# First mixer of a two-layer encoder: query and key blocks by seven half-size products, and GpSimd copies of x by halves

## The chip, the cores and the metric

One NeuronCore of a Trainium2 chip runs the whole kernel. The metric is the device time of one execution, in microseconds (us); less is better.

## The reference

The input x is 256 tokens of 1024 values, float32. Two layers follow, each a mixer with a residual add and then a mixture of experts with a residual add. The change lies in the first mixer, and there in its input projection:

```python
def even_mixer(xn, w_in, q_gain, k_gain, rel_bias, w_out):
    u = xn @ w_in                       # 256 x 1024 times 1024 x 2048
    q, k, v, ub = jnp.split(u, [NA_WIDTH, 2 * NA_WIDTH, 3 * NA_WIDTH], axis=-1)   # 512 each
    q = rms_norm(heads(q), q_gain)
    k = rms_norm(heads(k), k_gain)
    a = neighbourhood_attention(q, k, heads(v), rel_bias)
    b = fourier_mix(ub)
    return jnp.concatenate([a, b], axis=-1) @ w_out
...
x = x + even_mixer(rms_norm(x, ev_norm[i]), ...)
x = x + hier_moe(rms_norm(x, moe_norm[layer]), ...)    # 32 experts a layer, top 2 in the top group
```

## The kernel before

Large weights come as pieces of 2 MB, each 1024 x 512 values spread over 128 partitions (eight chunks of 128 rows, 512 columns each). Eleven slots in SBUF hold them. SyncE issues all of them in one fixed order: ident, the upper 128 tokens of x, w_in's piece 0 (query) in four parts with the lower 128 tokens of x ahead of the last, piece 1 (key, `w_k`), piece 2 (v, `w_v`), piece 3 (Fourier input, `w_u`), the two pieces of w_out, and then the pieces of layer 0's experts, each as soon as its slot is free. What frees a slot is a semaphore that SyncE waits for in the loop over `n` (L521 to L551): expert pieces 0 and 1 go where query and key weights lay, 2 and 3 where v and Fourier weights lay, piece 7 where scratch of the attention lay (after `s_o`), pieces 8 to 10 after the output projection, and piece 11 only after the first half of the first expert's gate has been multiplied. From there on a ring of eleven slots goes through the experts of layer 0, the six pieces of the second mixer, and the experts of layer 1.

The first mixer runs on all engines at once. TensorE transposes x by 128x128 blocks (`first_x_T`, upper tokens, then the lower ones after chunk 4 of the first block), VectorE scales the transposed chunks by the norm's gain into `xnT` (L937, L941), and TensorE multiplies them with the query piece (`first_block`) and the key piece (`dense_block`), 16 matmuls of 128x128 by 128x512 each: eight chunks for each half of the tokens. ScalarE and VectorE copy the four results out of PSUM with the row's 1/rms (L748, L1211).

The v and the Fourier piece are not multiplied block by block. With x cut into four quarters (two token halves, two halves of the 1024 inputs) and the weights into four (v or Fourier, two halves of the inputs), their four result blocks are made of seven products of quarter size instead of eight (the Strassen-Winograd scheme). Each product is four matmuls (`product`, L1722). It needs sums of x quarters, `XS[0]` to `XS[3]` (L1166 to L1171, 128x512 each), sums of weight quarters, T3, T1, T2, T4 (`weight_sums`, L1178 to L1184, 128x2048 each, VectorE), and sums of the products when they are read out of PSUM. `bank(b)` is one of the eight PSUM banks of 128x512 float32.

After the key block comes, for both blocks together: ScalarE's square of 128x2048 (L756), VectorE's sum over head elements (L1218), a root on ScalarE (L759), a reciprocal, and two multiplications that norm query and key (L1226). ScalarE copies the first v/Fourier product out only after its root (L762, L763), and the fourth product waits for that. Then transposes of query and key (L1453), three more products, scores, softmax, output projection, routing, experts.

GpSimd copies x from the landing area into its dealt order (L603) once both halves have landed, and issues the loads of the relative bias, 12 small ones (L613), after piece 3; when these have landed it adds the mask (L618). ScalarE issues four small loads of the query and key gains (L744) right after it has seen 1/rms ready, and the load of layer 0's constants (`lcst`, L751) behind its first copy.

## Time and profile before

| | |
|---|---|
| median of 3 runs | 1143.19 us (1143.02 to 1144.21) |
| the profiled execution | 1143.04 us |
| its span, first to last instruction | 1140.5 us |
| TensorE busy | 854.6 us (75%) |
| VectorE busy | 247.7 us (22%) |
| ScalarE busy | 169.0 us (15%) |
| moved by DMA | 439.26 MB, mean 385 GB/s |
| largest shares of the chain that ended last | DMA 54%, TensorE 39% |

The page counts busy time of each engine over the whole span, and follows one chain of work back from the last instruction. The profiled execution took 2.5 us more than its span, and is 0.15 us below the median of the runs. A matmul call in float32 shows as two records of TensorE (PE) with a weight load (PEld) each.

### The profile page before, as it was taken

The numbers are of one execution on the slowest core, as the hardware profiler recorded it, in microseconds if no ns is written. First come the engines' busy times: TensorE is split into PE (matmuls) and PEld (weight loads), VectorE is DVE, ScalarE is ACT, GpSimd is POOL, SyncE is SP. The second block draws the span as 40 slices with busy tenths as digits, with TensorE's granted clock in tenths as the row PEclk, the third lists the DMA queues.
The fourth block names the chain that finished last, engine by engine and source line by source line (L and its number), as shares of the span: only waits on it lengthen the run. The fifth ranks groups of instructions, "written<-read, shape, count | busy, mean of one in ns | idle before, by whom it ended". The sixth has DMA issues, their size and how long they took to land.

```text
span 1140.5 us, 20331 instructions
## 1 busy us (share of the span) xinstructions
PE 854.6 (75%) x9145; PEld 510.7 (45%) x9145; DVE 247.7 (22%) x790; ACT 169.0 (15%) x459; POOL 42.7 (4%) x48
## 2 busy tenths in 40 slices
PE   9999996656675757666899999966666675666666
PEld 4454663424343434333674556634343442434343
DVE  3651521111011111111234435211110021111111
ACT  2141210101011100001224232111010110101011
POOL 1561000000000000000000000000000000000000
PEclk9999998878889887878999999999787797888788
DMA  9994999999999999999992368999999999999997
GB/s 340 331 347 180 384 425 428 427 427 427 427 426 427 426 428 426 427 427 427 394 335 94 128 266 366 429 427 426 428 427 427 428 425 428 426 427 428 427 425 290
DMA packets 46869, 439.26 MB, mean 385 GB/s; under 512 B 4736, under 2 KB 5984, under 8 KB 21952
## 3 DMA queue, kind: packets, MB, share of 16 engines
q1 hardware_dynamic: 44240, 433.96, 91.3%
q0 software_dynamic: 1088, 2.97, 1.2%
q8 instruction: 72, 1.18, 0.4%
q10 hardware_dynamic: 1456, 1.04, 0.3%
q14 instruction: 13, 0.11, 0.0%
HBM read 436.91 MB, written 1.05 MB: 384 GB/s over the span
## 4 chain that ended last, share of the span: by engine, by line
DMA 54%; PE 39%; DVE 3%; SPq 1%; ACT 1%; issue 1%; POOL 0%; DVEq 0%; ACTq 0%
DMA mem<-in_moe_w_up 45%; PE psum L1446 34%; DMA mem<-in_moe_w_down 7%; PE psum L1610 2%; DMA mem<-in_ev_w_in 2%; PE psum L1722 1%; PE psum L1602 1%; PE psum L1625 1%; SPq L499 1%; PE psum L1463 0%; DVE mem L1054 0%; ACT mem L710 0%; DVE mem L1246 0%; DVE mem L1242 0%; PE psum L1805 0%
## 5 line engine op out<-in xcount | busy, mean ns | idle before, releaser
L1446 PE MATMUL psum<-mem 128*32 128x256 f32 (+6 forms) x7112 | 638.3, 432 | 262.8 <-DMA mem<-in_moe_w_up 224.5
L1446 PEld LDWEIGHTS psum<-mem 128*32 128x32 f32 (+2 forms) x7112 | 345.8, 132 | 525.5 <-issue 423.9
L1102 DVE TENSOR_TENSOR mem<-psum,mem 128x128 f32<-128x128 f32 x62 | 18.1, 291 | 639.6 <-ACT mem L724 622.5
L724 ACT ACTIVATE mem<-psum 128x128 f32<-128x128 f32 x62 | 17.2, 277 | 509.1 <-PE psum L1446 509.1
L1610 PE MATMUL psum<-mem 32*128 32x256 f32 x1024 | 73.4, 401 | 2.9 <-ACT mem L730 2.0
L1446 PE MATMUL psum<-mem,x 128*128 128x128 f32 (+1 forms) x512 | 64.0, 286 | 7.2 <-DVE mem L1054 3.7
L1446 PEld LDWEIGHTS psum<-mem,x 128*128 128x128 f32 x512 | 62.3, 203 | 8.8 <-DVE mem L1054 4.5
L1610 PEld LDWEIGHTS psum<-mem 32*128 32x128 f32 x1024 | 46.4, 184 | 30.6 <-issue 23.4
L1062 DVE TENSOR_SCALAR mem<-cst,mem 128x128 f32<-128x128 f32 x124 | 37.2, 342 | 20.7 <-PE psum L1602 20.7
L730 ACT COPY mem<-psum 128x256 f32<-128x256 f32 x62 | 23.1, 372 | 101.9 <-PE psum L1446 101.9
L726 ACT COPY mem<-psum 128x256 f32<-128x256 f32 x62 | 23.1, 372 | 66.4 <-PE psum L1602 66.3
L1602 PE MATMUL psum<-cst,mem 128*128 128x128 f32 x128 | 28.6, 306 | 3.2 <-ACT mem L710 3.2
L700 ACT ACTIVATE mem<-psum,g_dealt 128x128 f32<-128x128 f32 x64 | 18.2, 367 | 61.9 <-PE psum L1446 52.3
L1103 DVE STREAM_TRANSPOSE mem<-mem 128x128 f32<-128x128 f32 x62 | 25.1, 405 | 2.1
L1054 DVE TENSOR_SCALAR mem<-cst,mem,small 128x32 f32<-128x32 f32 x108 | 23.5, 295 | 7.4 <-PE psum L1610 7.4
L1722 PE MATMUL psum<-mem 128*128 128x512 f32 x56 | 24.6, 595 | 0.3 <-ACT mem L763 0.3
L1602 PEld LDWEIGHTS psum<-cst,mem 128*128 128x128 f32 x128 | 13.0, 143 | 23.9 <-issue 20.4
L1069 DVE TENSOR_SCALAR mem<-psum,g_dealt 128x128 f32<-128x128 f32 x64 | 18.0, 344 | 19.4 <-PE psum L1446 17.5
L648 POOL DMA_DIRECT2D mem<-in_c_layer x1 | 0.6, 598 | 460.4 <-PE psum L1446 460.4
L1722 PEld LDWEIGHTS psum<-mem 128*128 128x128 f32 x56 | 10.5, 191 | 13.6 <-issue 12.4
L638 POOL TENSOR_SCALAR mem<-mem 128x256 f32<-128x256 f32 x16 | 14.5, 921 | 14.1 <-DVE mem L1252 14.1
L1371 DVE SCALAR_TENSOR_TENSOR mem<-psum,mem 128x256 f32<-128x256 f32 (+1 forms) x32 | 11.1, 411 | 3.8 <-PE psum L1446 2.9
(198 smaller groups left out, 329.2 us busy)
## 6 DMA issues: line engine op xcount, KB each, us to landing
mem<-in_moe_w_gate SPq DMA_DIRECT2D x64, 2048.0 KB, 47.3
mem<-in_moe_w_up SPq DMA_DIRECT2D x64, 2048.0 KB, 48.4
mem<-in_moe_w_down SPq DMA_DIRECT2D x60, 2048.0 KB, 43.2
mem<-in_od_w_in SPq DMA_DIRECT2D x6, 2048.0 KB, 21.8
mem<-in_ev_w_in SPq DMA_DIRECT2D x3, 2048.0 KB, 19.0
mem<-in_moe_w_down SPq DMA_DIRECT2D x6, 1024.0 KB, 6.9
mem<-in_ev_w_out SPq DMA_DIRECT2D x2, 2048.0 KB, 25.0
mem<-in_od_w_out SPq DMA_DIRECT2D x2, 2048.0 KB, 21.0
```

Source lines behind the costliest of these rows:

```text
L700: nc.scalar.activation(xT_m[:, c], bank(6)[:, c * P:(c + 1) * P], ACT.Copy, scale=g_moe[l][:, c:c + 1]).then_inc(s["xT_a"], 1)
L726: nc.scalar.copy(M["GT"], bank(6)[:, 0:T]).then_inc(s["gtc"], 1)
L730: nc.scalar.copy(M["y"], bank(5)[:, 0:COLS]).then_inc(s["y"], 1)
L1054: ins = V.tensor_scalar(Ss_m[:, t, k], slotid[:, 0:CAP], rk3[:, t, e:e + 1], inv_rms(t), ALU.is_equal, ALU.mult)
L1062: V.tensor_scalar(Gs_m[:, t], slotid[:, 0:CAP].unsqueeze(1).broadcast_to([P, QUAD, CAP]), rk3[:, t, e:e + 1], G3[:, t, e:e + 1], ALU.is_eq ...
L1069: V.tensor_scalar(xT_m[:, c], bank(7)[:, c % 4 * P:(c % 4 + 1) * P], g_moe[l][:, c:c + 1], None, ALU.mult).then_inc(s["xT_v"], 1)
L1102: link(V.tensor_tensor(M["h"], src, M["sg"], ALU.mult))
L1103: V.transpose(hT_m, h_m).then_inc(done, 1)
L1446: return nc.tensor.matmul(out_, lhsT, rhs, start=start, stop=stop)
L1602: last = nc.tensor.transpose(bank(6)[:, t * P:(t + 1) * P], M["Gs"][:, t * P:(t + 1) * P], ident)
L1610: last = nc.tensor.matmul(bank(g)[:, t * COLS:(t + 1) * COLS], M["GT"][g * CAP:(g + 1) * CAP, t * P:(t + 1) * P], M["y"][g * CAP:(g + 1) * ...
L1722: last = nc.tensor.matmul(bank(b_), xs[:, c, :], w[:, c, :], start=first and c == 0, stop=True, skip_group_check=True)
```

## The change

The query and the key piece get the seven-product scheme too, so that both pairs of pieces run by it.

- TensorE: `first_products` multiplies only the upper tokens with the query piece, in two products of four matmuls (banks 4 and 5). Five products follow (banks 6, 7, 3, then 7 and 3 again on top), then the seven for v and Fourier as before.
- VectorE: the x sums move ahead of 1/rms and are formed from two differences, with `XS[3]` the sum of both; `XS[0]` and `XS[1]` come after the first weight sum. Four weight sums of 128x2048 are new: `TQ3` (in the area that v fills later), one into the key piece's lower half, two into the query piece. Seven scaled sums read the products out of PSUM (`qk_sum`), in place of two scaled copies; the last three of them stand between T1 and T2.
- ScalarE: two scaled copies of the first product (L752, L753) in place of the two copies of the blocks.
- SyncE: expert pieces 0 and 1 both wait for the seventh query/key product.
- GpSimd: the copy of x's upper half starts when that half has landed.

```diff
+        s_qp = sem("qk_product_done")
+        s_qr = sem("first_qk_product_copied")
+        s_qt = sem("qk_weight_sums_ready")
+        s_qd = sem("qk_product_read")
...
+        w_q, w_k = dense_slot("A", 0), dense_slot("A", 1)
+        TQ3 = A["vf"]
...
                 if n < 2:
-                    sp.wait_ge(used["A"], n + 1)
+                    sp.wait_ge(s_qp, 7)
                 elif n < 4:
...
-            pool.wait_ge(s_load["x"], 16)
-            pool.wait_ge(s_load["x_low"], 16)
             for t in range(TT):
+                pool.wait_ge(s_load["x_low" if t else "x"], 16)
                 pool.tensor_copy(x3[:, t].rearrange("p (c q) -> p c q", c=DC),
...
                                   a[name].rearrange("o d -> d o")).then_inc(s_load["qkgain"], 16)
-            for b in range(2):
-                act.wait_ge(used["A"], b + 1)
-                nc.scalar.activation(u_block(0, b), mbank(2 * b), ACT.Copy,
-                                     scale=inv_rms(0)).then_inc(s_ua["A"], 1)
-                if b == 0:
-                    act.dma_start(A["lcst"], a["c_layer0"]).then_inc(s_load["lc0"], 16)
-                if b == 1:
-                    act.wait_ge(s_ua["A"], 2)
-                    act.wait_ge(s_uv["A"], 2)
-                    nc.scalar.activation(A["sq"].rearrange("p (t n) -> p t n", t=TT), qk_a,
-                                         ACT.Square).then_inc(s_qsq, 1)
-                    act.wait_ge(s_qms, 1)
-                    nc.scalar.activation(A["st"][:, 0:32], A["st"][:, 0:32], ACT.Sqrt).then_inc(s_qrt, 1)
+            act.wait_ge(s_qp, 1)
+            nc.scalar.activation(u_block(0, 1), bank(4), ACT.Copy, scale=inv_rms(0)).then_inc(s_qr, 1)
+            nc.scalar.activation(u_block(1, 0), bank(4), ACT.Copy, scale=inv_rms(1)).then_inc(s_qr, 1)
+            act.dma_start(A["lcst"], a["c_layer0"]).then_inc(s_load["lc0"], 16)
+            act.wait_ge(s_qd, 7)
+            nc.scalar.activation(A["sq"].rearrange("p (t n) -> p t n", t=TT), qk_a, ACT.Square).then_inc(s_qsq, 1)
+            act.wait_ge(s_qms, 1)
+            nc.scalar.activation(A["st"][:, 0:32], A["st"][:, 0:32], ACT.Sqrt).then_inc(s_qrt, 1)
...
                     copy_bank(1)
+                if n == 0:
+                    x_sums()
                 dve.wait_ge(s_ssq, 2 * (n + 1))
...
                     copy_bank(3)
+                if n == 0:
+                    other_sums()
                 dve.wait_ge(s_rt, n + 1)
...
             dve.wait_ge(s_gc, 1)
+            def x_sums():
+                x1 = [xnT_of(0)[:, 0:DC // 2, t * P:(t + 1) * P] for t in range(TT)]
+                x2 = [xnT_of(0)[:, DC // 2:DC, t * P:(t + 1) * P] for t in range(TT)]
+                dve.wait_ge(s_xTv, DC + 2)
+                V.tensor_tensor(XS[2], x1[0], x1[1], ALU.subtract).then_inc(s_xs, 1)
+                V.tensor_tensor(XS[3], x2[0], x2[1], ALU.subtract).then_inc(s_xs, 1)
+                dve.wait_ge(s_xs, 2)
+                V.tensor_tensor(XS[3], XS[3], XS[2], ALU.add).then_inc(s_xs, 1)
+            def other_sums():
+                x1 = [xnT_of(0)[:, 0:DC // 2, t * P:(t + 1) * P] for t in range(TT)]
+                x2 = [xnT_of(0)[:, DC // 2:DC, t * P:(t + 1) * P] for t in range(TT)]
+                dve.wait_ge(*arrived["A", 1])
+                V.tensor_tensor(TQ3, w_k[:, hi], w_k[:, lo], ALU.subtract).then_inc(s_qt, 1)
+                V.tensor_tensor(XS[0], x1[1], x2[1], ALU.add).then_inc(s_xs, 1)
+                dve.wait_ge(s_xs, 4)
+                V.tensor_tensor(XS[1], XS[0], x1[0], ALU.subtract).then_inc(s_xs, 1)
             norm(0)
-            x1 = [xnT_of(0)[:, 0:DC // 2, t * P:(t + 1) * P] for t in range(TT)]
-            x2 = [xnT_of(0)[:, DC // 2:DC, t * P:(t + 1) * P] for t in range(TT)]
-            dve.wait_ge(s_xTv, DC + 2)
-            V.tensor_tensor(XS[0], x1[1], x2[1], ALU.add).then_inc(s_xs, 1)
-            V.tensor_tensor(XS[2], x1[0], x1[1], ALU.subtract).then_inc(s_xs, 1)
-            dve.wait_ge(s_xs, 1)
-            V.tensor_tensor(XS[1], XS[0], x1[0], ALU.subtract).then_inc(s_xs, 1)
-            dve.wait_ge(s_xs, 3)
-            V.tensor_tensor(XS[3], x2[0], XS[1], ALU.subtract).then_inc(s_xs, 1)
-            def weight_sums():
+            def qk_sum(to, b_, t, add, n):
+                dve.wait_ge(s_qp, n)
+                V.scalar_tensor_tensor(to, bank(b_), inv_rms(t), add, ALU.mult, ALU.add).then_inc(s_qd, 1)
+            dve.wait_ge(s_qt, 1)
+            dve.wait_ge(s_qp, 1)
+            V.tensor_tensor(w_k[:, lo], TQ3, w_q[:, lo], ALU.add).then_inc(s_qt, 1)
+            dve.wait_ge(s_qr, 2)
+            qk_sum(u_block(0, 0), 5, 0, u_block(0, 1), 2)
+            qk_sum(u_block(0, 1), 6, 0, u_block(0, 1), 3)
+            qk_sum(u_block(1, 1), 7, 1, u_block(1, 0), 4)
+            dve.wait_ge(s_qt, 2)
+            V.tensor_tensor(w_q[:, hi], w_q[:, hi], w_k[:, lo], ALU.subtract).then_inc(s_qt, 1)
+            qk_sum(u_block(1, 0), 3, 1, u_block(1, 0), 5)
+            V.tensor_tensor(w_q[:, lo], w_k[:, hi], w_k[:, lo], ALU.subtract).then_inc(s_qt, 1)
+            def weight_sums(between):
...
                 V.tensor_tensor(TS["T1"], w_v[:, lo], w_u[:, lo], ALU.subtract).then_inc(s_ts, 1)
+                between()
                 dve.wait_ge(s_ts, 2)
...
                     continue
-                dve.wait_ge(used["A"], b + 1)
-                V.tensor_scalar(u_block(1, b), mbank(2 * b + 1), inv_rms(1), None,
-                                ALU.mult).then_inc(s_uv["A"], 1)
                 if b == 0:
-                    weight_sums()
+                    def last_qk_sums():
+                        dve.wait_ge(s_qd, 4)
+                        qk_sum(u_block(1, 0), 7, 1, u_block(1, 0), 6)
+                        qk_sum(u_block(0, 1), 3, 0, u_block(0, 1), 7)
+                        qk_sum(u_block(1, 1), 3, 1, u_block(1, 1), 7)
+                    weight_sums(last_qk_sums)
                 if b == 1:
...
                     link(V.reciprocal(st[:, 32:64], st[:, 0:32]))
-                    dve.wait_ge(s_ua["A"], 2)
                     for t in range(TT):
...
-            def first_block(b0):
-                w = dense_slot("A", 0).rearrange("p (c n) -> p c n", c=DC)
+            def first_products():
+                w = w_q.rearrange("p (c n) -> p c n", c=DC)
                 first_x_T(0)
-                for t in range(TT):
-                    for c in range(DC):
-                        if t == 0:
-                            pe.wait_ge(s_xTv, c + 1)
-                            if c % 2 == 0:
-                                pe.wait_ge(*((s_first[c // 2], 16) if c < 6 else arrived["A", 0]))
-                        elif c % 4 == 0:
-                            pe.wait_ge(s_xTv, DC + c // 4 + 1)
-                        last = mm(bank(b0 + t), xnT_of(0)[:, c, t * P:(t + 1) * P], w[:, c, :], c == 0, c == DC - 1)
-                        if t == 0 and c == 4:
-                            first_x_T(1)
-                last.then_inc(used["A"], 1)
+                for c in range(DC):
+                    pe.wait_ge(s_xTv, c + 1)
+                    if c % 2 == 0:
+                        pe.wait_ge(*((s_first[c // 2], 16) if c < 6 else arrived["A", 0]))
+                    last = mm(bank(4 + c // 4), xnT_of(0)[:, c, 0:P], w[:, c, :], c % 4 == 0, c % 4 == 3)
+                    if c % 4 == 3:
+                        last.then_inc(s_qp, 1)
+                    if c == 4:
+                        first_x_T(1)
...
             nc.tensor.transpose(mbank(3)[:, 0:G_ROWS], g_rows[0:G_ROWS, :], ident[0:G_ROWS, 0:G_ROWS]).then_inc(s_gr, 1)
-            first_block(4)
-            dense_block("A", 1, xnT_of(0), 6)
-            pe.wait_ge(s_gc, 1)
-            pe.wait_ge(s_xTv, DC + 2)
+            first_products()
             x_lo = [xnT_of(0)[:, 0:DC // 2, t * P:(t + 1) * P] for t in range(TT)]
...
+            pe.wait_ge(*arrived["A", 1])
+            pe.wait_ge(s_xs, 3)
+            product(6, XS[3], w_k[:, hi], True).then_inc(s_qp, 1)
+            pe.wait_ge(s_gc, 1)
+            pe.wait_ge(s_qt, 1)
+            product(7, XS[2], TQ3, True).then_inc(s_qp, 1)
+            pe.wait_ge(s_xs, 5)
+            pe.wait_ge(s_qt, 2)
+            product(3, XS[1], w_k[:, lo], True).then_inc(s_qp, 1)
+            pe.wait_ge(s_qt, 3)
+            pe.wait_ge(s_qd, 3)
+            product(7, x_hi[1], w_q[:, hi], False).then_inc(s_qp, 1)
+            pe.wait_ge(s_qt, 4)
+            pe.wait_ge(s_qd, 4)
+            product(3, XS[0], w_q[:, lo], False).then_inc(s_qp, 1)
             pe.wait_ge(*arrived["A", 3])
             product(0, x_lo[0], w_u[:, lo], True).then_inc(s_pp, 1)
-            pe.wait_ge(s_xs, 4)
             pe.wait_ge(s_ts, 1)
...
             product(2, x_hi[1], TS["T4"], False).then_inc(s_pp, 1)
-            pe.wait_ge(s_uv["A"], 3)
+            pe.wait_ge(s_uv["A"], 1)
             product(1, XS[3], w_v[:, hi], False).then_inc(s_pp, 1)
...
                 if c == 0:
-                    pe.wait_ge(s_ua["A"], 3)
-                    pe.wait_ge(s_uv["A"], 4)
+                    pe.wait_ge(s_ua["A"], 1)
+                    pe.wait_ge(s_uv["A"], 2)
                     pe.wait_ge(s_load["lc0"], 16)
...
                     pe.wait_ge(s_f2c, 2)
-                    pe.wait_ge(s_uv["A"], 5)
+                    pe.wait_ge(s_uv["A"], 3)
                 else:
...
```

On VectorE, behind the scaled chunks of x, these rows stood before (`x_sums_ready` counts sums of x, `landed_1` to `landed_3` the pieces, `weight_sums_ready` the sums T1 to T4):

```order
L1169 TENSOR_TENSOR mem<-mem 128x512 [waits x_sums_ready]
L1171 TENSOR_TENSOR mem<-mem 128x512 [waits x_sums_ready]
L1211 TENSOR_SCALAR mem<-psum,small 128x512 [waits used_A]
L1178 TENSOR_TENSOR mem<-mem 128x2048 [waits x_dealt,landed_3,landed_2]
L1180 TENSOR_TENSOR mem<-mem 128x2048 [waits weight_sums_ready]
L1182 TENSOR_TENSOR mem<-mem 128x2048 [waits weight_sums_ready]
L1184 TENSOR_TENSOR mem<-mem 128x2048 [waits weight_sums_ready]
L1211 TENSOR_SCALAR mem<-psum,small 128x512 [waits used_A]
L1218 TENSOR_REDUCE mem<-mem 128x32 [waits qk_squared]
L1219 TENSOR_SCALAR mem<-mem 128x32 [waits dve_chain]
L1221 RECIPROCAL mem<-mem 128x32 [waits qk_root]
```

and these stand in the changed kernel, from the first weight sum on (`qk_product_done` counts the seven products, `qk_weight_sums_ready` the four new sums), with the last five rows in a fence of their own:

```order
L1180 TENSOR_TENSOR mem<-mem 128x2048 [waits landed_1]
L1181 TENSOR_TENSOR mem<-mem 128x512
L1183 TENSOR_TENSOR mem<-mem 128x512 [waits x_sums_ready]
L956 RECIPROCAL small<-small 128x2 [waits root_ready]
L1194 TENSOR_TENSOR mem<-mem 128x2048 [waits qk_product_done,qk_weight_sums_ready,inv_rms_ready]
L1190 SCALAR_TENSOR_TENSOR mem<-psum,small,mem 128x512 [waits qk_product_done,first_qk_product_copied]
L1190 SCALAR_TENSOR_TENSOR mem<-psum,small,mem 128x512 [waits qk_product_done] x2
L1200 TENSOR_TENSOR mem<-mem 128x2048 [waits qk_weight_sums_ready]
L1190 SCALAR_TENSOR_TENSOR mem<-psum,small,mem 128x512 [waits qk_product_done]
L1202 TENSOR_TENSOR mem<-mem 128x2048
L1209 TENSOR_TENSOR mem<-mem 128x2048 [waits x_dealt,landed_3,landed_2]
L1211 TENSOR_TENSOR mem<-mem 128x2048 [waits weight_sums_ready]
```

```order
L1190 SCALAR_TENSOR_TENSOR mem<-psum,small,mem 128x512 [waits qk_product_done,qk_product_read]
L1190 SCALAR_TENSOR_TENSOR mem<-psum,small,mem 128x512 [waits qk_product_done] x2
L1214 TENSOR_TENSOR mem<-mem 128x2048 [waits weight_sums_ready]
L1216 TENSOR_TENSOR mem<-mem 128x2048 [waits weight_sums_ready]
L1255 TENSOR_REDUCE mem<-mem 128x32 [waits qk_squared]
```

Four rows of 128x2048 and the readouts of seven products have come in ahead of the sum over squares (L1218 before, L1255 now), and the reciprocal that makes 1/rms now stands behind a wait for piece 1.

On ScalarE, from its root of the mean square on, before:

```order
L677 ACTIVATE small<-small 128x2 [waits mean_square_ready]
L744 DMA small<-in_ev_q_gain 64x1 [waits inv_rms_ready]
L744 DMA small<-in_ev_q_gain 64x1
L744 DMA small<-in_ev_k_gain 64x1 x2
L748 ACTIVATE mem<-psum,small 128x512 [waits used_A]
L751 DMA mem<-in_c_layer 128x964
L748 ACTIVATE mem<-psum,small 128x512 [waits used_A]
L756 ACTIVATE mem<-mem 128x2048 [waits u_copied_dve_A,u_copied_act_A]
L759 ACTIVATE mem<-mem 128x32 [waits qk_mean_square]
L762 ACTIVATE mem<-psum,small 128x512 [waits uv_product_done]
```

and now:

```order
L682 ACTIVATE small<-small 128x2 [waits mean_square_ready]
L749 DMA small<-in_ev_q_gain 64x1 [waits inv_rms_ready]
L749 DMA small<-in_ev_q_gain 64x1
L749 DMA small<-in_ev_k_gain 64x1 x2
L752 ACTIVATE mem<-psum,small 128x512 [waits qk_product_done]
L753 ACTIVATE mem<-psum,small 128x512
L754 DMA mem<-in_c_layer 128x964
L756 ACTIVATE mem<-mem 128x2048 [waits qk_product_read]
L758 ACTIVATE mem<-mem 128x32 [waits qk_mean_square]
L761 ACTIVATE mem<-psum,small 128x512 [waits uv_product_done]
```

The two copies of the first product stand behind the four small loads as the first copy did before, but VectorE's first readout now waits for them.

On TensorE, before, from the key block to the fourth v/Fourier product:

```order
L1446 MATMUL psum<-mem 128x512 [waits landed_1]
L1446 MATMUL psum<-mem 128x512 x15
L1722 MATMUL psum<-mem 128x512 [waits landed_3,xnT_copied,gains_copied]
L1722 MATMUL psum<-mem 128x512 x3
L1722 MATMUL psum<-mem 128x512 [waits weight_sums_ready,x_sums_ready]
L1722 MATMUL psum<-mem 128x512 x3
L1722 MATMUL psum<-mem 128x512 [waits weight_sums_ready]
L1722 MATMUL psum<-mem 128x512 x3
L1722 MATMUL psum<-mem 128x512 [waits first_product_copied]
```

and now, from the last chunks of the query product to the first v/Fourier product:

```order
L1482 MATMUL psum<-mem 128x512 [waits xnT_copied]
L1752 MATMUL psum<-mem 128x512 [waits x_sums_ready,landed_1]
L1752 MATMUL psum<-mem 128x512 x3
L1752 MATMUL psum<-mem 128x512 [waits qk_weight_sums_ready,gains_copied]
L1752 MATMUL psum<-mem 128x512 x3
L1752 MATMUL psum<-mem 128x512 [waits qk_weight_sums_ready,x_sums_ready]
L1752 MATMUL psum<-mem 128x512 x3
L1752 MATMUL psum<-mem 128x512 [waits qk_product_read,qk_weight_sums_ready]
L1752 MATMUL psum<-mem 128x512 x3
L1752 MATMUL psum<-mem 128x512 [waits qk_product_read,qk_weight_sums_ready]
L1752 MATMUL psum<-mem 128x512 x3
L1752 MATMUL psum<-mem 128x512 [waits landed_3]
```

Behind the products on piece 0, everything now waits for piece 1 (`landed_1`), and each of the next four products for a sum of VectorE.

## Rows read from the trace of the kernel before

**Rows 1.** The page: what DMA moved in each of 40 slices of 28.5 us.

```profile
GB/s 340 331 347 180 384 425 428 427 427 427 427 426 427 426 428 426 427 427 427 394 335 94 128 266 366 429 427 426 428 427 427 428 425 428 426 427 428 427 425 290
```

**Rows 2.** SyncE's queue in order of time: start, us of issue, what.

```profile
4.34 10.64 SPq L474 DMA_DIRECT2D mem<-in_ev_w_in  x3
...
27.74 6.33 SPq L481 DMA_DIRECT2D mem<-in_moe_w_gate  x1
...
62.38 0.33 SPq L481 DMA_DIRECT2D mem<-in_moe_w_down  x1
...
104.04 0.33 SPq L481 DMA_DIRECT2D mem<-in_moe_w_up  x1
...
128.42 0.33 SPq L491 DMA_DIRECT2D mem<-in_moe_w_down  x1
```

**Rows 3.** Stretches: length, busy PE, PEld, DVE, ACT, POOL, then clock, DMA share, GB/s.

```profile
92.00:104.00 12.00, 12.00 (x44) 5.45 (x43) 0.84 (x2) 2.65 (x4) 1.60 (x2) 1.00 0.01 1
...
190.00:197.00 7.00, 5.89 (x59) 3.24 (x63) 0.00 (x0) 0.00 (x0) 0.00 (x0) 0.51 0.99 419
...
200.00:500.00 300.00, 192.97 (x2496) 116.25 (x2494) 39.91 (x142) 27.92 (x89) 0.00 (x0) 0.84 1.01 427
```

**Rows 4.** The chain that ended last, from 30 to 47 us: start, us, what.

```profile
30.66 2.30 DVE mem L1178
...
39.93 0.67 DVE mem L1211
...
40.69 1.92 ACT mem L756
...
42.63 2.30 DVE mem L1218
...
45.39 0.58 ACT mem L762
```

**Rows 5.** TensorE in order of time, 12 to 50 us.

```profile
12.62 23.34 PE L1446 MATMUL psum<-mem 128*128 128x512 f32 x54
35.80 10.46 PE L1722 MATMUL psum<-mem 128*128 128x512 f32 x24
46.60 3.70 PE L1722 MATMUL psum<-mem 128*128 128x512 f32 x8 [0.34 <-ACT mem L763]
```

**Rows 6.** DMA issued before 4.5 us: the large one, KB, us to landing.

```profile
mem<-in_ev_w_in SPq DMA_DIRECT2D x1, 2048.0 KB, 14.1
```

**Rows 7.** VectorE in order of time, 14 to 50 us.

```profile
14.55 1.79 DVE L1166 TENSOR_TENSOR mem<-mem 128x512 f32<-128x512 f32 x1
16.27 0.68 DVE L1167 TENSOR_TENSOR mem<-mem 128x512 f32<-128x512 f32 x1
16.87 0.68 DVE L1169 TENSOR_TENSOR mem<-mem 128x512 f32<-128x512 f32 x1
...
45.81 2.36 DVE L1226 TENSOR_TENSOR mem<-mem 128x1024 f32<-128x1024 f32 x2
48.09 0.74 DVE L1230 SCALAR_TENSOR_TENSOR mem<-psum,small,mem 128x512 f32<-128x512 f32 x1
48.75 0.74 DVE L1232 SCALAR_TENSOR_TENSOR mem<-psum,small,mem 128x512 f32<-128x512 f32 x1
```

**Rows 8.** ScalarE's queue: the four small loads.

```profile
14.55 1.18 ACTq L744 DMA_DIRECT2D small<-in_ev_q_gain  x2
15.75 1.27 ACTq L744 DMA_DIRECT2D small<-in_ev_k_gain  x2
```

**Rows 9.** GpSimd in order of time.

```profile
11.76 4.04 POOL L603 COPY x<-mem 128x1024 f32<-128x1024 f32 x2 [11.32 <-DMA mem<-in_x]
...
50.02 6.69 POOL L618 TENSOR_TENSOR mem<-mem 128x3072 f32<-128x3072 f32 x1 [10.77 <-DMA mem<-in_ev_rel_bias]
```

**Rows 10.** TensorE among the experts, after waits of 3 to 4 us.

```profile
355.62 3.66 PE L1446 MATMUL psum<-mem 128*32 128x256 f32 x64 [3.26 <-DMA mem<-in_moe_w_up]
...
1039.23 5.35 PE L1446 MATMUL psum<-mem 128*32 128x256 f32 x64 [3.71 <-issue]
```

2 lines of the change are left out of this document (1 added, 1 removed).

## The prediction

> **What bounds the kernel now.** I read the page first. DMA moves 427 GB/s in nearly every slice; the exceptions are the two mixers and what lies between them [rows 1]. From 200 to 500 us the DMA engines are full while TensorE works 193 of 300 us [rows 3], so the experts are bound by their weights, and the end is the number of bytes at 427 GB/s plus the time in which nothing moves. The first mixer makes such time: SyncE can't issue expert piece 7 before 104.04 us or piece 11 before 128.42 us [rows 2], and from 92 to 104 us DMA stands still while TensorE is busy without a break [rows 3]. Both issues wait for the mixer, or for the first expert behind it. So each microsecond by which the mixer ends earlier or later moves the whole stream after it, and the end, by the same microsecond. Faster or slower work elsewhere in the first 100 us counts only if it moves that end.
>
> What sets the mixer's end stands in the chain of waits. From 30.66 us it runs on VectorE, not on TensorE: four weight sums up to 39.93, the key block's copy, ScalarE's square, the sum over heads from 42.63, a root, and ScalarE's two copies of the first v/Fourier product from 45.39 [rows 4]. TensorE, which had worked from 12.62 us on, waits 0.34 us for these and starts the fourth product at 46.60 [rows 5]. All that follows hangs on that start; the change leaves it alone. So I ask one thing: **when does the fourth v/Fourier product start in the changed kernel?**
>
> **TensorE.** 54 records from 12.62 to 35.80 us are 27 matmuls, 0.86 us each [rows 5]. Four of 32 go: 3.4 us less. But the query's second half-block and 16 matmuls on the key piece used to fill the time. Now, after chunks 5 to 7 (12.62 + 3 x 0.86 = 15.2, some 0.2 later by the copy below), nothing is left that doesn't need piece 1. It was issued first of three at 4.34 us [rows 2] and landed 14.1 us later [rows 6], at 18.44. TensorE idles 3.1 us, most of the gain. By TensorE alone the fourth product could start at 18.5 + 8 x 3.44 = 46.0 (five query/key and three v/Fourier products of 3.44), 0.6 us earlier. That is the best the change could do.
>
> **VectorE.** It can't keep that pace. A sum of 128x2048 takes (39.93 - 30.66) / 4 = 2.32 us from start to start [rows 4]; one of 128x512 0.60, or its full 0.68 and a wake-up (0.71) if the next waits for it, and a scaled sum out of PSUM 0.66 [rows 7]. From piece 1 on:
> - `TQ3` 18.50 to 20.82, two x sums (0.71 + 0.60) to 22.14, 1/rms 0.2 to 22.34. The reciprocal used to be done at 14.5 and now stands behind the wait for piece 1.
> - ScalarE starts its four small loads only then. They hold its queue for 2.47 us [rows 8], to 24.8; its two copies of the first product take 0.58 each [rows 4], to 26.05. VectorE meanwhile makes the key piece's sum (to 24.66) and waits 1.4 us.
> - Three scaled sums, 1.98, to 28.07 (the third product to be read ends at 25.4). Sum into the query piece to 30.4; TensorE, through at 28.8, waits 1.6 us for it. Scaled sum 0.66, next weight sum 2.32, to 33.37.
> - T3 and T1 to 38.02. Piece 3, which bound them before, has been there since 30.6. Last three scaled sums to 40.0, T2 and T4 to 44.66. ScalarE's square of 1.92 [rows 4] starts at 40.0 and is hidden under T2 and T4.
> - The sum over heads starts at 44.66; before it was 42.63 [rows 4]. From there on nothing differs.
>
> So the fourth product starts at 46.60 + 2.03 = 48.63. TensorE would be ready at 47.6: its last query/key products run from 30.4 to 37.3, and three more make 47.6. As a sum: eight weight sums 18.6, x sums and reciprocal 1.5, seven scaled sums 4.6, the wait 1.4, together 26.2 us from 18.50, against 12.0 us from 30.66 before: 14.2 us more work, begun 12.2 us earlier.
>
> **Costed at nothing.** Expert pieces 0 and 1 are both issued at 37.5, the first instead of at 27.74 [rows 2]; w_out and the bias loads are ahead of them and keep DMA busy till about 50, so no gap opens, and the first expert needs them after 120 us. If the seventh product came 10 us later, DMA would starve. Constants load 4 us later; their reader comes 20 us later still. T3's scratch wait and x's copies: GpSimd's copy of the upper half now runs from 5.1 to 7.1 us, alongside VectorE's small sum of two SBUF operands (L1160 before). L1166 shows what that does: 1.79 us instead of 0.68, ended right behind GpSimd's copies [rows 7, 9]. So the first scaled chunk slips from 6.3 to about 7.2, and TensorE by 0.2 to 0.3 us, covered by the 3.1 us for piece 1.
>
> **The sum.** 1143.04 (the profiled execution; 0.15 under the median) + 2.03 = **1145.1 us**. Its own uncertainty is 0.6 us: a dozen steps rounded, waits of 0.02 to 0.1 us between engines, how ScalarE's loads fall.
>
> **Rivals.**
> - *The small loads don't hold ScalarE.* In the trace a load (L751) started together with a copy, so its queue runs ahead of the engine; here the loads stand ahead of the copy, and I take them as in its way. If not, VectorE's 1.4 us go: +0.6, 1143.7. Chance 0.10.
> - *GpSimd's bias addition gets in between the two multiplications that norm query and key.* This is the slower side. GpSimd's addition reads two SBUF operands for 6.69 us from 50.02 [rows 9]. The second multiplication of L1226 started at 45.81 + 1.18 = 47.0, 3 us ahead of it [rows 7]; moved by 2.03 it starts at 49.0, and the constants' later load lets piece 3 and with it the bias land up to 0.6 us earlier, at 49.4. If the addition is first, the multiplication waits for its end at 56.1, as L1166 did, and ends at 57.3 instead of 50.2. TensorE, which would transpose from 52.3, starts 5.0 us later: +7.0, 1150.1. It decides at a margin of 0.4 to 1.0 us. Chance 0.12.
>
>   The Trainium skill's GPSIMD Engine Reference, section "Key points", says that GpSimd shares its SBUF interfaces with VectorE and contends with instructions that read two SBUF operands; by that rule the same thing happens, and L1166 agrees with it.
> - *TensorE's clock falls in its wait for piece 1.* After a wait of 3.26 us 64 matmul records took 3.66 us, after one of 3.71 they took 5.35 [rows 10]; this wait is 3.1. The longest such stretch I found is 190 to 197 us: a granted clock of 0.51, the 1.2 GHz level, over 5.9 busy us [rows 3]. If TensorE worked 5.5 us at that level after the wait, it would lose 2.8 us; VectorE's third scaled sum would slip 0.9, the next sums 0.5 more: +3.4, 1146.5. Chance 0.08.
> - *TensorE's work is what counts*, and the 3.4 us of four matmuls reach the end: 1139.6. For that VectorE's sums and piece 1's landing would both have to be off the path. Chance 0.04.
>
> **How the numbers follow.** The forecast has the remaining 0.66. A measurement of this kernel tells 0.2% from no change, 2.3 us here: 1140.9 to 1145.5 around the median. The forecast lies inside, 0.4 us under the upper edge; with 0.6 us of its own, about a quarter falls outside: 0.49 within, 0.17 slower. Rival one is within (0.10), two and three are slower (0.20), four is faster (0.04). Together: faster 0.04, same 0.59, slower 0.37. The range goes from rival one, 1143.6, to past the clock's case, 1147.2; it leaves out rivals two and four and a little at each end.
>
> **What would show it.** Right: TensorE idle from 15.4 to 18.5 us, then some 1.6 us ahead of the product on `x_hi[1]`, VectorE nearly without a gap from 18.5 to 47 but for about 1.4 us behind its second weight sum, ScalarE's small loads from 22.3, the fourth v/Fourier product at 48.6, piece 7 issued at 106.1 and piece 11 at 130.5 us. VectorE's first two-operand sum would take about 1.6 us instead of 0.19. Wrong: a fourth product ahead of 47 us; a multiplication of query and key of more than 2 us; piece 7 moved by another amount than that product; or a shift in the mixer that the experts don't keep.

## The result, and the profile after

| | before | after |
|---|---|---|
| median of 14 runs each, alternating | 1143.07 us (1142.74 to 1144.21) | 1147.86 us (1143.61 to 1152.25) |
| ratio, 95% interval | | 1.0042 (1.0027 to 1.0057): slower, by the 0.2% that the prediction counts as a change |
| the profiled execution | 1143.04 us | 1144.03 us |
| its span | 1140.5 us | 1142.0 us |

The median of after is a number that hardly any run has. Its 14 runs are 1143.61, 1143.96, 1144.03, 1144.61, 1144.95, 1145.04, 1145.36 and then 1150.36, 1150.95, 1151.74, 1151.83, 1152.07, 1152.12, 1152.25: seven and seven, with 5 us of nothing between. The runs of before all lie within 1.5 us. With seven runs in each group the median is the mean of 1145.36 and 1150.36; one run more in the lower group would have made it 1145.36. The profiled execution is one of the lower group. So there are two questions: what costs the lower group its 1.5 us, and what adds 7 us to half of the executions.

The lower group's part is plain from the profile. VectorE in order of time, from the x sums on (start, us, engine, line, operation; for a row of several the us are those of all):

```profile
5.58 1.93 DVE L1163 TENSOR_TENSOR small<-cst 128x36 f32<-128x36 f32 x1
...
18.19 2.29 DVE L1180 TENSOR_TENSOR mem<-mem 128x2048 f32<-128x2048 f32 x1 [1.91 <-DMA mem<-in_ev_w_in]
20.40 0.68 DVE L1181 TENSOR_TENSOR mem<-mem 128x512 f32<-128x512 f32 x1
21.12 0.69 DVE L1183 TENSOR_TENSOR mem<-mem 128x512 f32<-128x512 f32 x1
21.73 0.16 DVE L956 RECIPROCAL small<-small 128x2 f32<-128x2 f32 x1
21.92 2.29 DVE L1194 TENSOR_TENSOR mem<-mem 128x2048 f32<-128x2048 f32 x1
25.74 2.07 DVE L1190 SCALAR_TENSOR_TENSOR mem<-psum,small,mem 128x512 f32<-128x512 f32 x3 [1.52 <-ACT mem L753]
27.72 2.28 DVE L1200 TENSOR_TENSOR mem<-mem 128x2048 f32<-128x2048 f32 x1
...
43.81 2.28 DVE L1255 TENSOR_REDUCE mem<-mem 128x32 f32<-128x2048 f32 x1
...
46.99 2.36 DVE L1262 TENSOR_TENSOR mem<-mem 128x1024 f32<-128x1024 f32 x2
```

and TensorE:

```profile
13.10 2.74 PE L1482 MATMUL psum<-mem 128*128 128x512 f32 x6
18.21 10.57 PE L1752 MATMUL psum<-mem 128*128 128x512 f32 x24 [2.38 <-DMA mem<-in_ev_w_in]
30.06 17.43 PE L1752 MATMUL psum<-mem 128*128 128x512 f32 x40 [1.28 <-DVE mem L1200]
47.77 3.70 PE L1752 MATMUL psum<-mem 128*128 128x512 f32 x8 [0.28 <-ACT mem L762]
51.31 1.91 PE L1489 MATMUL psum<-cst,mem 128*128 128x128 f32 x16
```

TensorE now idles 2.38 us for piece 1 and 1.28 us for VectorE's sum, and the fourth v/Fourier product starts at 47.77 instead of 46.60 [rows 5]: 1.17 us later. SyncE's queue shows what becomes of that, against 104.04 and 128.42 [rows 2]:

```profile
105.21 0.33 SPq L487 DMA_DIRECT2D mem<-in_moe_w_up  x1
...
129.59 0.33 SPq L497 DMA_DIRECT2D mem<-in_moe_w_down  x1
```

Both issues are 1.17 us later, the same as the product. An issue near 1090 us is 1.27 later, the last ones (the output) 1.46: 1.17 of the 1.46 come from the mixer, the rest arises among the experts and differs between executions (see the part on the prediction). The time of the profiled execution grew by only 0.99 us, since before took 2.5 us more than its span and after 2.0; why, no run shows.

What the half of the executions hangs on stands on GpSimd:

```profile
29.56 8.32 POOL L618 DMA_DIRECT2D mem<-in_ev_rel_bias  x12 [16.06 <-DMA mem<-in_ev_w_in]
48.43 7.48 POOL L623 TENSOR_TENSOR mem<-mem 128x3072 f32<-128x3072 f32 x1 [10.55 <-DMA mem<-in_ev_rel_bias]
```

The bias addition (L618 before, L623 now) is ready at 48.43 us, not at 50.02 [rows 9]. The second of the two multiplications of L1262 starts at about 46.99 + 1.18 = 48.17 us (an estimate: half of the pair's 2.36; the view of this line says 48.1). That leaves some 0.26 us between them, where before it was 3.0. Here the multiplication was first, and the addition took 7.48 us instead of 6.69: it did not get on until the multiplication ended at 49.35. If the order of the two turned round, the multiplication would wait for the whole addition. The first experiments test that.

### The profile page after: what moved, and what is told of

It reads as the page before. It is cut to its first block, busy times and chain, and to the rows that moved or that the text cites. A ratio compares the mean times of both kernels' runs of the same rounds, so it can differ in the third digit from the quotient of the medians.

```text
span 1142.0 us, 20327 instructions
## 1 busy us (share of the span) xinstructions
PE 850.1 (74%) x9137; PEld 506.7 (44%) x9137; DVE 260.8 (23%) x800; ACT 169.1 (15%) x459; POOL 43.5 (4%) x48
## 3 DMA queue, kind: packets, MB, share of 16 engines
q8 instruction: 72, 1.18, 0.4%
## 4 chain that ended last, share of the span: by engine, by line
DMA 53%; PE 39%; DVE 4%; ACT 1%; SPq 1%; issue 1%; ACTq 0%; POOL 0%; DVEq 0%
DMA mem<-in_moe_w_up 44%; PE psum L1482 34%; DMA mem<-in_moe_w_down 7%; PE psum L1643 2%; PE psum L1752 1%; DMA mem<-in_ev_w_in 1%; PE psum L1635 1%; PE psum L1658 1%; SPq L505 1%; DVE mem L1190 0%; PE psum L1499 0%; DVE mem L1057 0%; ACT mem L715 0%; DVE mem L1282 0%; DVE mem L1278 0%
## 5 line engine op out<-in xcount | busy, mean ns | idle before, releaser
L1482 PE MATMUL psum<-mem 128*32 128x256 f32 (+3 forms) x7064 | 615.5, 429 | 265.2 <-DMA mem<-in_moe_w_up 231.9
L1482 PEld LDWEIGHTS psum<-mem 128*32 128x32 f32 (+1 forms) x7064 | 333.7, 130 | 516.9 <-issue 413.9
L1643 PEld LDWEIGHTS psum<-mem 32*128 32x128 f32 x1024 | 46.2, 184 | 30.7 <-issue 23.5
L1752 PE MATMUL psum<-mem 128*128 128x512 f32 x96 | 42.2, 595 | 3.9 <-DMA mem<-in_ev_w_in 2.4
L1635 PE MATMUL psum<-cst,mem 128*128 128x128 f32 x128 | 28.5, 305 | 3.3 <-ACT mem L715 3.3
L1752 PEld LDWEIGHTS psum<-mem 128*128 128x128 f32 x96 | 17.9, 190 | 27.5 <-issue 20.8
```

The costliest lines, as they stand in the source:

```text
L1482: return nc.tensor.matmul(out_, lhsT, rhs, start=start, stop=stop)
L1635: last = nc.tensor.transpose(bank(6)[:, t * P:(t + 1) * P], M["Gs"][:, t * P:(t + 1) * P], ident)
L1643: last = nc.tensor.matmul(bank(g)[:, t * COLS:(t + 1) * COLS], M["GT"][g * CAP:(g + 1) * CAP, t * P:(t + 1) * P], M["y"][g * CAP:(g + 1) * ...
L1752: last = nc.tensor.matmul(bank(b_), xs[:, c, :], w[:, c, :], start=first and c == 0, stop=True, skip_group_check=True)
```

## The experiments

In each, the first theory is that the upper group consists of executions in which the addition starts ahead of the second multiplication. "A run like 1151" means one of the upper group. Each experiment alternated with runs of the kernel before: these had medians of 1143.26 us (29 runs) beside experiments 1 to 4, 1143.62 (33) beside 5 to 8 and 1143.81 (23) beside 9 to 11, and each ratio is against its own.

**1. The addition waits for both multiplications.**

```diff
             pool.wait_ge(s_load["lc0"], 16)
+            pool.wait_ge(s_qn, 2)
```

> The changed kernel, with one wait more: GpSimd's bias addition (L623) starts only after both multiplications that norm query and key. Theory L (the runs near 1151 us are those in which this addition starts between the two multiplications and holds up the second until it ends): no run near 1151, all between 1143.5 and 1145.5; the addition runs from 49.3 to about 56 us and its reader comes at 64.7, so the wait costs nothing. Rival C (those runs come from TensorE's clock falling in its wait for piece 1) or D (from how the DMA engines serve piece 1): half of the runs stay near 1151.

Measured: 1144.63 us (1143.63 to 1145.68, 11 runs), ratio 1.0011 (1.0002 to 1.0020). No run was above 1145.7. The addition starts at 49.54 and takes its 6.69 us, the fourth product starts at 47.78, piece 11 at 129.61: the lower group, and nothing else. What the change costs without the collision is this 0.1%.

**2. The addition is made to come first.** The two readouts of v and Fourier products (reads of PSUM) go ahead of the two multiplications, which moves the multiplications by 2 us.

```diff
-                    for t in range(TT):
-                        qk = qk_a[:, t].rearrange("p (g d) -> p g d", d=NA_DH)
...
                     V.scalar_tensor_tensor(u_block(1, 3), bank(1), inv_rms(1), r1_low, ALU.mult, ALU.add).then_inc(s_ps, 1)
+                    for t in range(TT):
+                        qk = qk_a[:, t].rearrange("p (g d) -> p g d", d=NA_DH)
...
```

> The changed kernel, with VectorE's two readouts out of PSUM (L1266, L1268) ahead of the two multiplications that norm query and key, so that the addition on GpSimd (start 48.4 us in the profile) is always first. Theory L: all runs near 1150 to 1152; in the profile the first multiplication lasts over 5 us and ends right behind GpSimd's addition at 55.2 us, both are done near 56.4, TensorE's transposes start there instead of at 51.3, and TensorE's clock shows 0.5 for some us after that wait of 5 us. Rivals C and D: the mix of 1144 and 1151 stays as it was.

Measured: 1152.39 us (1151.36 to 1153.68, 5 runs), ratio 1.0080 (1.0067 to 1.0093). Every run is now an upper one. VectorE's rows:

```profile
47.72 0.75 DVE L1262 SCALAR_TENSOR_TENSOR mem<-psum,small,mem 128x512 f32<-128x512 f32 x1 [0.97 <-ACT mem L762]
48.39 0.74 DVE L1264 SCALAR_TENSOR_TENSOR mem<-psum,small,mem 128x512 f32<-128x512 f32 x1
49.05 7.62 DVE L1268 TENSOR_TENSOR mem<-mem 128x1024 f32<-128x1024 f32 x2
```

GpSimd's, with the addition started first and in its usual time:

```profile
47.79 6.66 POOL L623 TENSOR_TENSOR mem<-mem 128x3072 f32<-128x3072 f32 x1 [9.88 <-DMA mem<-in_ev_rel_bias]
```

TensorE's, and the table of stretches with its granted clock (the third number from the right):

```profile
47.58 3.70 PE L1752 MATMUL psum<-mem 128*128 128x512 f32 x8 [0.29 <-ACT mem L762]
56.73 3.67 PE L1489 MATMUL psum<-cst,mem 128*128 128x128 f32 x16 [5.45 <-DVE mem L1268]
```

```profile
48.00:52.00 4.00, 3.27 (x8) 1.14 (x6) 4.00 (x3) 0.69 (x1) 4.00 (x1) 1.00 1.10 441
52.00:56.00 4.00, 0.00 (x0) 0.00 (x0) 4.00 (x2) 0.00 (x0) 4.00 (x4) 0.88 1.01 430
56.00:60.00 4.00, 3.27 (x16) 3.28 (x17) 2.59 (x4) 0.00 (x0) 4.00 (x7) 0.50 0.99 348
60.00:64.00 4.00, 4.00 (x9) 1.82 (x8) 1.09 (x2) 0.00 (x0) 1.63 (x3) 0.77 0.78 97
64.00:70.00 6.00, 6.00 (x15) 2.66 (x14) 1.50 (x2) 0.00 (x0) 0.00 (x0) 1.00 0.01 2
```

Three things are to be seen. The multiplications took 7.62 us instead of 2.36 and ended 2.2 us behind the addition's end at 54.45, the time of the two of them. The two readouts, one operand of which is in PSUM, took their 0.75 and 0.74 us although the addition ran beside them. And TensorE, having waited 5.45 us, came back at a granted clock of 0.50 (1.2 GHz): 16 transposes took 3.67 us instead of 1.91, and the clock rose again only after 60 us. Expert piece 11 went out at 137.56 us, 7.95 later than in experiment 1: 5.4 from the hold-up (the transposes start at 56.73 instead of 51.32), and 2.5 from the clock (the transposes and the 24 records of products behind them take 14.69 us until the next kind starts, instead of 12.15). Also, the addition was ready at 47.79 here, where it was at 48.43 in the profile of after, although its loads were issued at 29.59 and 29.56. The edit moves nothing ahead of 46 us, so I take this as what the landing varies by between executions, and it is more than the margin of 0.26.

**3. Both edits.** If the moved readouts and not the addition cost the time, it stays slow.

> Both edits: the readouts first, and GpSimd's addition after both multiplications. Control for the forced order: theory L expects 1143.5 to 1145.5 in all runs, the order of VectorE alone costing 0.3 us at most (multiplications 49.2 to 51.5 against transposes that could start at 51.3). If the order itself cost the time, near 1151.

Measured: 1145.57 us (1144.04 to 1146.04, 11 runs), ratio 1.0017 (1.0009 to 1.0026). The multiplications start at 49.08 and take 2.35 us, the addition starts at 51.62, piece 11 goes out at 129.84. So it is the order of addition and multiplication that costs the 7 us; the moved readouts cost 0.2 us of piece 11's issue against experiment 1 (0.4 counted from the fourth product, which started at 47.61 here) and 0.9 of the median, where 0.3 at most was expected. The other half of the 0.9 is not explained.

The Trainium skill's page "SBUF — State Buffer", section "SBUF: two separate sides", says that the pair shared by VectorE and GpSimd is an exclusive lock and that whichever instruction starts first gets it for the whole instruction. The traces agree in both directions: 7.62 us against 2.36, and 7.48 against 6.69. In the four traces in which the addition started during the second multiplication (after and experiments 4, 9 and 10) the two overlap by 0.92, 0.27, 1.00 and 0.24 us, and the addition is 0.79, 0.14, 0.86 and 0.10 us longer than 6.69: each time the overlap less 0.13 or 0.14.

**4. 1/rms first.** The reciprocal goes ahead of the wait for piece 1, so that the small loads are through ScalarE's queue before the first product is.

```diff
-                if n == 0:
-                    other_sums()
                 dve.wait_ge(s_rt, n + 1)
                 V.reciprocal(small[:, 14:16], small[:, 12:14]).then_inc(s_rs, 1)
+                if n == 0:
+                    other_sums()
```

> The changed kernel, with 1/rms computed ahead of VectorE's wait for piece 1, as before the change; no guard. VectorE's wait of 1.5 us for ScalarE's copies (25.74 us) goes and the fourth v/Fourier product starts at about 46.2 us instead of 47.8; layer constants load 4 us earlier again, so that piece 3 and the bias land later (addition near 50 us instead of 48.4). Theory L: the second multiplication starts at 46.6, over 3 us ahead of the addition, and no run is near 1151; median 1142.6. If the two groups come from something else, both stay, each 1.5 us lower.

Measured: 1145.47 us (1142.65 to 1146.05, and one run of 1329.32, left out of the ratio: its mean granted clock was 0.59, where the others have 0.87 to 0.89, and why is open; 12 runs), ratio 1.0010 (1.0001 to 1.0018). Of the other 11 runs none is an upper one, though the addition was ready at 49.37 and the second multiplication started at 48.46: a margin of 0.91 us, not the 3 expected. It did what it should to ScalarE: reciprocal at 16.33, small loads at 16.52, copies at 19.04, and VectorE's wait of 1.5 us for them is gone. But the median is 2.9 us above what was expected (1142.6), and the fourth product started at 48.06 instead of 46.2, later than in after. TensorE's and VectorE's rows and TensorE's stretches say why:

```profile
18.15 29.18 PE L1752 MATMUL psum<-mem 128*128 128x512 f32 x64 [2.54 <-DMA mem<-in_ev_w_in]
48.06 2.41 PE L1752 MATMUL psum<-mem 128*128 128x512 f32 x5 [0.73 <-ACT mem L762]
```

```profile
26.77 0.75 DVE L1190 SCALAR_TENSOR_TENSOR mem<-psum,small,mem 128x512 f32<-128x512 f32 x1 [1.49 <-PE psum L1752]
...
30.20 0.75 DVE L1190 SCALAR_TENSOR_TENSOR mem<-psum,small,mem 128x512 f32<-128x512 f32 x1 [0.48 <-PE psum L1752]
```

```profile
15.00:18.00 3.00, 0.61 (x2) 0.00 (x0) 1.19 (x4) 0.20 (x1) 0.00 (x0) 0.95 1.05 386
18.00:19.00 1.00, 0.85 (x1) 0.50 (x2) 0.87 (x1) 0.00 (x0) 0.00 (x0) 0.50 1.06 389
19.00:20.00 1.00, 1.00 (x2) 0.34 (x1) 1.00 (x1) 0.96 (x2) 0.00 (x0) 0.50 1.06 389
20.00:21.00 1.00, 1.00 (x3) 0.47 (x2) 1.00 (x2) 0.30 (x1) 0.00 (x0) 0.50 1.04 371
21.00:22.00 1.00, 1.00 (x4) 0.52 (x3) 0.96 (x3) 0.00 (x0) 0.00 (x0) 0.95 1.08 367
```

After the wait for piece 1 the clock stood at 0.50 for some 3 us. In the profile of after, which waited 2.38 us at the same place, it stayed at 1.00. TensorE worked without a pause from piece 1 to 47.33, and its slowed products came late to VectorE, which waited 1.49 and 0.48 us for them; from 30.20 on VectorE has no gap up to the sum over heads, and through it and ScalarE's root the late products set the fourth one. This is one execution. Its output was issued 2.93 us later than in before, of which only 1.47 stand at piece 11; the rest came among the experts, after 750 us.

**5. Experiment 4, with the wait filled.** Two matmuls whose result nobody reads (the bank is overwritten next) run before the wait.

```diff
             first_products()
+            for _ in range(2):
+                mm(bank(6), xnT_of(0)[:, 7, 0:P], w_q[:, 7 * 512:8 * 512])
```

> e4 (1/rms first) with two more matmuls of 128x512 on TensorE behind the first two products, into a bank that the next product overwrites: they fill 1.7 of the 2.5 us in which TensorE waits for piece 1. Theory C (the spread of e4, from 1142.7 to 1146.0, and part of the spread of e1, is the clock that falls in that wait in some runs, as e4's profile shows: 0.50 from 18 to 21 us): the clock stays at 1.00 from 15 to 30 us, the fourth v/Fourier product starts at 46.6 us, and all runs lie between 1142.3 and 1144.0. If the spread comes from elsewhere (the DMA engines, the experts), it stays at 3 us and the median near 1145.

Measured: 1143.70 us (1142.62 to 1145.08, 11 runs), ratio 0.9998 (0.9989 to 1.0007): with these two edits the changed kernel can't be told from the kernel before. No run is an upper one, at a margin of 2.1 us (addition ready at 49.11). The runs reach 1145.08, where 1144.0 was expected as the highest. The clock is 1.00 from 15 to 30 us, the fourth product starts at 46.59, piece 11 goes out at 128.43, each within 0.01 us of before. Yet this profiled execution took 1143.97 us, 0.9 more than that of before. The difference arises at the second mixer, 16 transposes before it and here:

```profile
556.54 1.98 PE L1463 MATMUL psum<-cst,x 128*128 128x128 f32 x16 [1.23 <-DVEq L1153]
```

```profile
556.54 3.63 PE L1499 MATMUL psum<-cst,x 128*128 128x128 f32 x16 [1.23 <-DVEq L1156]
```

Same start, same wait of 1.23 us, but a clock of 0.58 instead of 1.00 from 556 to 560 us. This costs 1.3 us in some executions and not in others, in a part that no edit touches; of the 13 traces it shows in this one and in that of experiment 8. It is likely part of what spreads the runs of before over their 1.5 to 2.9 us; no run was made to show that. That the two matmuls are what kept the clock up in the first wait is not shown either: without them it stayed at 1.00 in the traces of after and of experiments 1, 2, 3, 6, 9 and 10. Fewer runs are high here than in experiment 4, which fits.

**6. Are GpSimd's copies by halves worth anything?** Experiment 1, with both copies after both halves again.

> e1 (bias addition after the norm) with GpSimd's copy of x undone: both halves after the lower one has landed, as before the change. VectorE's small two-operand sum takes 0.19 us instead of 1.93, the first product starts at 7.3 instead of 7.8 us and TensorE is through at 15.4 instead of 15.8; piece 1 lands at 18.2 as before. Expected by the prediction's costing: no difference from e1 (median within 0.5 us), unless the longer wait for piece 1 makes the clock fall more often (up to +1).

Measured: 1144.60 us (1143.84 to 1148.21, 11 runs), ratio 1.0014 (1.0004 to 1.0024), against 1.0011 in experiment 1. The two-operand sum at 5.58 takes 0.18 us instead of 1.93, but then the copies (11.58, 4.03 us) hold up an x sum at 13.81 (2.35 us instead of 0.69). Both delays end ahead of piece 1, and the fourth product starts at 47.83. Three runs, at 1147.09, 1148.15 and 1148.21, belong to neither group; their cause stays open.

**7. All mended.** Experiment 5, with the guard of experiment 1, and ScalarE's two copies of the first v/Fourier product ahead of its root, since experiment 5's TensorE waited 0.73 us for them.

```diff
-            act.wait_ge(s_qms, 1)
-            nc.scalar.activation(A["st"][:, 0:32], A["st"][:, 0:32], ACT.Sqrt).then_inc(s_qrt, 1)
...
             nc.scalar.activation(r1_low, bank(0), ACT.Copy, scale=inv_rms(1)).then_inc(s_r1, 1)
+            act.wait_ge(s_qms, 1)
+            nc.scalar.activation(A["st"][:, 0:32], A["st"][:, 0:32], ACT.Sqrt).then_inc(s_qrt, 1)
```

> e5 with the bias addition held back as in e1, and ScalarE's two copies of the first v/Fourier product ahead of its root instead of behind it. The fourth product then waits for TensorE alone: it starts at 18.2 + 8 x 3.44 = 45.7 us, 0.9 before the kernel before the change (46.60). Expected 1142.2 us, all runs within 1 us. If the root's place did not matter, 1143.0.

Measured: 1142.46 us (1141.47 to 1145.05, 11 runs), ratio 0.9991 (0.9982 to 1.0000). TensorE runs from piece 1 to its transposes without a break:

```profile
18.42 31.17 PE L1755 MATMUL psum<-mem 128*128 128x512 f32 x72 [1.12 <-DMA mem<-in_ev_w_in]
49.42 1.91 PE L1490 MATMUL psum<-cst,mem 128*128 128x128 f32 x16
```

72 records are nine products of 3.44 us. They can't start before piece 1 is there, so 49.4 is the floor of this arrangement, and piece 11 goes out 0.70 us earlier than before. The runs spread over 3.6 us, not over the 1 expected. The new place of ScalarE's copies was not tried in the kernel before, whose fourth product waited 0.34 us for them [rows 5]; so up to that much of the gain may not be owed to the change.

**8. Piece 1 in two halves.** The third query/key product needs only the upper half of the key piece. It is loaded first, with a semaphore of its own, and the filling is left out.

```diff
+                    sp.dma_start(dst[:, DC // 2:DC], src[:, DC // 2:DC]).then_inc(s_khi, 16)
+                    sp.dma_start(dst[:, 0:DC // 2], src[:, 0:DC // 2]).then_inc(arrived["A", j][0], 16)
...
-            pe.wait_ge(*arrived["A", 1])
+            pe.wait_ge(s_khi, 16)
```

> e7 without the filling matmuls, and with piece 1 loaded in two halves, the upper input half first: the third product needs only that half. It lands near 15.5 us, so TensorE goes on at 16.2 (when the third x sum is ready), the fourth query/key product starts when its weight sum is ready (20.5 us, was 21.6), and the fourth v/Fourier product at about 44.6 us, 2.0 ahead of the kernel before. Expected 1141.1 us. If the mixer's end did not set the end of the kernel one to one, less than 2 us.

Measured: 1142.40 us (1141.15 to 1143.82, 11 runs), ratio 0.9988 (0.9979 to 0.9997): 1.2 us faster than before, the same as experiment 7 within 0.1, and 1.3 above the 1141.1 expected. The third product starts at 16.03. Waits of 0.79 and 0.41 us for VectorE's sums come back, and piece 11 goes out at 127.09, 1.33 us earlier than before and not the 2 expected. The profiled execution is the slowest of the 11 all the same (1143.82 us): the 16 transposes of the second mixer ran at a low clock, as in experiment 5,

```profile
555.55 3.46 PE L1507 MATMUL psum<-cst,x 128*128 128x128 f32 x16 [1.23 <-DVEq L1163]
```

and another microsecond went among the experts of layer 1.

**9. The changed kernel again**, beside experiments 10 and 11.

> The changed kernel once more, beside the others of this call. Theory L: again two groups of runs, near 1144 and near 1151, with nothing between 1146.5 and 1150; if the profile falls into the upper group, one of the two multiplications of L1262 lasts over 5 us. If chip and day made the two groups, there is one only.

Measured: 1144.08, 1144.09, 1150.65, 1151.79, 1151.92 and 1152.01 us; ratio of the median of 1151.22 us: 1.0057 (1.0037 to 1.0078). With the first 14 that is 11 of 20 in the upper group. Its profile was of the lower one once more, with the addition at 48.27 and the second multiplication at 48.09.

**10. The constants' load ahead of the small ones.** In the changed kernel, layer 0's constants are issued 2.2 us later than before (24.49 against 22.27 us), and may so come to stand behind piece 3's transfer; piece 3 and the bias would then land earlier.

```diff
+            act.dma_start(A["lcst"], a["c_layer0"]).then_inc(s_load["lc0"], 16)
             for k, name in enumerate(("ev_q_gain", "ev_k_gain")):
...
-            act.dma_start(A["lcst"], a["c_layer0"]).then_inc(s_load["lc0"], 16)
```

> The changed kernel, with ScalarE's load of layer 0's constants ahead of its four small loads (issued near 22 us, as before the change, instead of 24.5). Nothing else: no guard, 1/rms still behind piece 1. Theory: these constants had come to stand behind piece 3 instead of ahead of it, which let piece 3 and the bias land 1.1 to 1.6 us earlier (bias loads issued at 29.56 instead of 30.87, addition at 48.4 instead of 50.0). Put back, the addition starts near 49.7 us and the second multiplication near 48.6: no run near 1151, median 1145. If the margin was lost by the later norm alone, the upper group stays.

Measured: 1144.93 us (1144.09 to 1153.22, 12 runs), ratio 1.0018 (1.0004 to 1.0031). With the constants issued at 21.71, the bias loads go out at 30.46 instead of 29.56 and the addition is ready at 49.28 instead of 48.43; the second multiplication starts at 48.34. The margin is 0.94 us instead of 0.26, and one run of 12 (1153.22) is an upper one instead of 11 of 20. The traces of all kernels fall apart by this: where the constants go out by 22.7 us (seven traces), the bias loads are issued from 30.43 to 30.87 and the addition is ready from 49.02 to 50.02; where they go out after 24.2 (six), the loads are issued from 29.52 to 29.81, and the addition is ready from 47.79 to 48.43 in the three that show it. So of the 2.8 us by which the margin shrank, 1.2 are the later multiplication and 1.6 the earlier landing. Moving the one load back returns 0.85 of these 1.6, and the mean landings of the two sorts of traces (49.38 and 48.16) differ by 1.2; the rest is what executions differ by. No run near 1151 was expected, and there is one: it is counted as an upper run by its time alone. One more run, at 1147.17, is of neither group.

**11. The copies by halves alone, in the kernel before.**

```diff
-            pool.wait_ge(s_load["x"], 16)
-            pool.wait_ge(s_load["x_low"], 16)
             for t in range(TT):
+                pool.wait_ge(s_load["x_low" if t else "x"], 16)
```

> The kernel before, with GpSimd's copy of x's upper half started as soon as that half has landed, and nothing else. VectorE's small two-operand sum (L1160) is held up until GpSimd's copy ends, near 7.1 us, so the first block starts 0.5 us later; TensorE is busy without a break from there to 46 us, but the fourth v/Fourier product waits for VectorE's chain from piece 3 on. Expected: no difference (1143.1), at most +0.3.

Measured: 1142.90 us (1142.39 to 1143.81, 11 runs), ratio 0.9996 (0.9987 to 1.0004). The two-operand sum grows to 1.88 us as in after, and piece 11 goes out 0.19 us earlier. No difference can be measured, here or in experiment 6.

## Why the prediction was wrong

The forecast was 1145.1 us in a range to 1147.2; the median is 1147.86, and it is slower, to which I gave 0.37.

**The step that failed** is rival two, "GpSimd's bias addition gets in between the two multiplications": its chance of 0.12, and that this chance was given as if one execution decided it for all. The mechanism was named rightly, and the margin was near the lower end of "0.4 to 1.0 us" (some 0.26 in the profile of after). But two terms of that margin were wrong and nearly cancelled, which is luck. The bias was to land "up to 0.6 us earlier", at 49.4; it came 1.6 earlier, at 48.43, some half of that or more because the constants' load goes out later (experiment 10). The second multiplication was to start at 49.0; it started at 48.17. The profile of before was a poor base besides: its 50.02 is the latest of seven such landings. What the margin should have been held against is what landings vary by: 47.79, 48.27 and 48.43 in three traces of the same arrangement. With a margin as small as that the order falls out anew in every execution: 11 of 20 runs were upper ones, against 1 of 12 at 0.94 us, 0 of 11 at 0.91, and 0 of 11 at 2.1. With half of the runs in each group the median falls anywhere between 1144.6 and 1151.8; that it came out at 1147.86, outside the range, and not at 1145.36, inside, was one run's doing. The mixture was none of my rivals, and the range ends below it.

The rival's price was too low as well. It was +7.0 over before: 2.03 of mixer shift and 5.0 of hold-up, 1150.1 in all. The upper group's median is 1151.83, 8.8 over before, and 7.2 over the lower group (7.8 from experiment 1 to 2), where 5.0 was forecast. The hold-up itself was right, 5.4 in experiment 2; what was left out are the 2.5 us of TensorE's clock, which fell in the longer wait. The mixer shift of 1.17 instead of 2.03 hides a part of that.

**The rest of the chain**, for the lower group, point by point:

- *The end moves with the fourth v/Fourier product, one to one*: right up to piece 11 in every trace but those of experiments 2 and 3, whose edits lie behind the product. The product and piece 11 moved by +1.17 and +1.17 in after, by −0.01 and +0.01 in experiment 5; for 7 and 8, where the product is no longer a mark of its own, the transposes moved by −0.72 and −1.33, piece 11 by −0.70 and −1.33. The medians follow piece 11 within some 0.9 us (−1.16 and −1.22 for 7 and 8). A single execution need not: from piece 11 to the issue of the output the shift grew from 0.01 to 1.38 us in the trace of experiment 5, from −1.33 to 1.27 in 8, from 1.35 to 2.29 in 10 and from 1.47 to 2.93 in 4, and stayed within 0.6 in the other eight.
- *The product starts at 48.63*: it was 47.77, so the term of +2.03 measured +1.17. Piece 1 was there at 18.2, not 18.5. A sum of 128x2048 takes 2.20 us from start to start when the next doesn't wait for its result (18.19 to 20.40, 27.72 on); I used 2.32 for all, which came from four sums of which three wait [rows 4]. On five or so of the eight sums that is 0.6 us.
- *VectorE, not TensorE, sets it*: right. TensorE's waits (2.38 for piece 1, 1.28 for VectorE's sum) were forecast as 3.1 and 1.6, and it waits 0.28 us for ScalarE's copy ahead of the fourth product.
- *Small loads hold ScalarE's copies, 1.4 us for VectorE*: right, 1.52 measured, the loads from 21.92 to 24.39 and the first copy at 24.44. Rival one falls with it. Experiment 4 takes the wait away.
- *VectorE's first two-operand sum takes 1.6 us instead of 0.19 beside GpSimd's copy, and TensorE slips 0.2 to 0.3*: 1.93 us; the last chunks of the query product started 0.48 us later (13.10 against 12.62), hidden by piece 1 as said.
- *Constants' later load, costed at nothing*: they went out 2.2 us later, not 4, and landed by 31.3 us; but this brought the bias forward, by 0.85 us as far as experiment 10 shows.
- *The clock falls in the wait for piece 1, +3.4, if the wait is long*: it did not fall in the profile of after (2.38 us), nor after 2.81 us at the same place in experiment 6, nor after 3.26 us in the kernel before [rows 10], and it fell in experiment 4's profile after 2.54. So the length of the wait does not decide it alone. Its price was near 1.5 us, the fourth product at 48.06 instead of 46.59.
- *TensorE's saved 3.4 us reach the end*: no. The mixer ends 0.7 to 1.3 us earlier only after the mends of experiments 7 and 8; until then piece 1's landing and VectorE's new sums take them.

What I did not show: no execution of the changed kernel itself out of the upper group was profiled; its cause rests on experiment 2, which forces the order, on experiments 1 and 3, which forbid it, and on 10, which widens the margin. The changed kernel did not run beside experiments 1 to 8, so that it would have shown its two groups there too is taken from the 14 runs and from experiment 9. And 7 us cannot be told apart exactly into hold-up and clock for those runs.

## What to carry to other kernels

Where VectorE has an instruction with two operands in SBUF and GpSimd one that reads SBUF, write down both start times and the gap between them, before and after a change; a gap of 0.26 us, with a landing behind one of the two, was a coin tossed in every execution, one of 0.9 us still lost one run in 23, and one wait on a semaphore settled it for nothing (1144.63 against the lower group's 1144.61). Ask of each load that a change issues later what then lands earlier. And before forecasting a median, ask if the runs can fall in two groups: one profile shows one group, and here both profiles of the changed kernel showed the one that hides most of the loss.

## What the runs showed of the hardware

- In these traces a VectorE instruction of two SBUF operands that meets a running GpSimd instruction that reads SBUF stops until that one is through (128x36: 1.93 us instead of 0.18; two of 128x1024: 7.62 instead of 2.36), and the GpSimd addition that starts second is longer by nearly the whole overlap (7.48 instead of 6.69). A readout with one operand in PSUM was not held up (0.74 us beside the addition, 0.74 alone).
- TensorE's granted clock fell to 0.50 after a wait of 2.54 us in one execution and stayed at 1.00 after 2.38, 2.81 and 3.26 us in others; near 556 us it fell in 2 of the 13 profiled executions (to 0.58 over 4 us in experiment 5), with the same work and the same wait of 1.23 us before it. It is a source of 1 to 1.5 us between executions of one kernel.
- One run of experiment 4, at 1329 us with a mean granted clock of 0.59, and four runs near 1147 to 1148 us in experiments 6 and 10 have no cause that I can name.
